# One core, one hybrid block: table powers in PSUM, a table shared with GpSimd, tokens turned unscaled, and the last third of w_mod in column halves

## The chip, the cores and the metric

The kernel runs on one core of a Trainium2 chip. The metric is the device time of one execution in microseconds (us); where several runs were made, their median stands. Beside it there is one profiled execution, whose trace gives every duration that is quoted below. Times "at 83 us" count from the start of that execution's span.

Engines are named as the trace names them: PE is TensorE, DVE is VectorE, ACT is ScalarE, POOL is GpSimd, SP is the engine that here only issues transfers (SPq in the trace).

## The reference, cut to what matters

```python
mod_x = silu(c) @ w_mod + b_mod            # 6 x 1024 values; the same from c_ctx for the context
hx = rmsnorm(x) * (1 + sc1) + sh1          # 256 latent tokens, 256 context tokens, width 1024
ux = hx @ w_in                             # columns 0:512 pooling mixer, 512:1024 SSM
# SSM: 32 groups of 16 channels, 64 complex states, forward and backward, over chunks of 8 tokens
ssm = gelu(readout(scan(ux_ssm)) + d*ux_ssm);  ssm = ssm * sigmoid(ssm @ w_glu + b_glu)
pool = (centred_mean(ux_pool) - ux_pool) @ w_pool * s_pool
x = x + g1 * (concat(pool, ssm) @ w_out)
hx2 = rmsnorm(x) * (1 + sc2) + sh2
eidx, gate = route(hx2)                    # best group of 8 experts, its top 2 of 32 experts in all
x = x + g2 * moe(hx2, eidx, gate)          # w_gate, w_up (1024x512), w_down (512x1024) per expert
return rmsnorm(x) * g_final
```

Everything is float32. The 32 experts' weights are 6 MB each; all of them are read, four experts in each of eight passes.

## The kernel before, in words

Each engine has its own program, written out by hand, and runs it in order; waits on named semaphores order the engines against each other. All large loads go through SP's queue, in the order of SP's program. The work falls into these stages.

**Tables.** The scan over tokens is done in chunks of L = 8 tokens. DVE makes the powers of the 2 x 16 diagonal factors (LP), copies them into PW (a tile of SBUF, `pws`), and multiplies them with the input matrices Br into the table SA and, later and with other powers, with the output matrices CT into the table MO. `powers_times` does this: a table has four parts (direction d, real or imaginary part rr), each made in two halves h, and a half is three instructions over 128x1024 elements: a product into SBUF, a product into PSUM, and the two combined. So SA and MO have eight halves each. POOL makes MO's d = 1, real part, in two halves. PE turns (transposes) SA in sixteen pieces, `turn_sa`, each four 128x128 transposes; ACT copies them into ST (DVE three of them). `lag_kernels(d)` multiplies SA with CT.

**Modulation and first projection.** Meanwhile PE multiplies silu(c) with the first third of w_mod, eight chunks of 1 MB, sums in PSUM bank 4. When all eight are in, ACT copies the row (`mod_rows`), PE turns it, ACT makes columns of it (`mod_columns`), POOL makes the scale A1. PE turns the normed tokens piece by piece (`turn_x`), ACT evacuates each piece with scale and shift into hT, and `u_ssm(q)`, q = 0 to 3, multiplies hT with w_in's SSM half. The turns of x (k = 3 to 7) stand inside `u_ssm(0)`, eight turns of SA inside `u_ssm(1)`.

**States and scan.** `u_evacuate(q)` writes u to DRAM; SP reads it back in another layout (U8, two halves of eight transfers). `state_inputs(0)` and `(1)` multiply it with ST, ACT copies the results, and DVE scans them from then until `hp_ready`. After the last `state_inputs` SP issues w_out's pool half and 15 transfers that build the Toeplitz matrix TT, then the chunks 6 and 7 of w_mod's second third. PE does the pooling projection `u_pool` and the chunks between them, then the windows, w_pool, the Toeplitz product, `mix_pool(0)`, and, with `hp_ready`, the readout y.

**To the residual.** y is copied, turned, put through gelu and the gated unit, and multiplied with w_out (`mix_mm`, four pieces). The last third of w_mod (scale 2, gate 2) is summed on DVE instead of PE: `mod_sum(k)`, one instruction over 128x2048 for each of eight chunks, into `acc`. PE sums acc over the partitions with a matrix of ones, and adds the bias with a second product: the scale half (`scale_mm`) after the second piece of mix_mm, the gate half (`gate_mm`) after the router's logits. From scale_mm DVE makes A2b, the norm's scale, before the first residual.

**Experts.** After the router, `gather` brings tokens to slots. DVE counts passes (`passes_ready`), and each engine loads that number into a register before its loop of four experts. SP's loads of the loop wait until PE has used the buffer. Weights of the first experts are loaded into free buffers before that.

Of the kernel before, what the change touches and what calls it, by code (L numbers as in the profile page):

```python
# [7 lines left out]
ALU = mybir.AluOpType  # L8
# [8 lines left out]
L = 8  # L17
# [41 lines left out]
def hybrid_block(nc, x, ctx, w_mod, columns, ssm_bc, b_mod_rows, w_in, w_out, w_pool, w_glu, w_router, b_router,  # L59
# [14 lines left out]
    with ExitStack() as stack:  # L74
# [22 lines left out]
        pws = sb("pws", 512)  # L97
# [17 lines left out]
        wm0 = wm + [wts[:, 20480:22528], wts[:, 22528:24576], ra[:, 4096:6144], ra[:, 6144:8192], wm[0]]  # L115
# [34 lines left out]
        PW = pws[:, :].rearrange("p (d r g s) -> p d r g s", d=2, r=2, g=GP)  # L150
# [70 lines left out]

        u_dram = nc.dram_tensor("u_scratch", [P, 2048], F32).ap()
# [31 lines left out]
        def _(sp):  # L254
# [55 lines left out]
            sp.dma_start(wglu, w_glu[0].rearrange("(k p) n -> p k n", p=P)).then_inc(S("wglu_in"), 16)  # L310
            sp.dma_start(wo_ssm, w_out_v[:, 4:8, :]).then_inc(S("wo_ssm_in"), 16)
            for k in range(3):
                mod_chunk(2, k)
            sp.wait_ge(S("gff_row"), 16)
            sp.dma_start(gffb, row_dram[1:2, 0:D].broadcast_to([P, D])).then_inc(S("gff_in"), 16)
            sp.wait_ge(S("mod1_row"), 16)
            sp.dma_start(ra[:, 6144:8192], row_dram[0:1].broadcast_to([P, 2048])).then_inc(S("g1_in"), 16)
            sp.wait_ge(S("pool_mm"), 1)
            mod_chunk(2, 3)

            sp.wait_ge(S("hp_ready"), 1)
            mod_chunk(2, 4)
# [3 lines left out]
            mod_chunk(2, 5)  # L326
            gu_load(sp, 0, 0, 0, "up")
            gu_load(sp, 0, 0, 1, "up")
            mod_chunk(2, 6)
            for half in range(2):  # L330
                down_load(sp, lambda j: j, half, (1,))
            mod_chunk(2, 7)
# [3 lines left out]
            sp.wait_ge(S("mod2_used"), KD)  # L336
            gu_load(sp, 0, 0, 0, "gate")
            gu_load(sp, 0, 0, 1, "gate")
# [48 lines left out]
        def _(gp):  # L387
# [21 lines left out]
            gp.wait_ge(S("mod_col"), 1)  # L409
            gp.tensor_tensor(A1, MC[:, 1, :, :], vt[:, V_GM:V_GM + 8].unsqueeze(2).broadcast_to([P, KD, 2]),  # L410
# [1115 lines left out]
```

## Time and profile before

| what | value |
|---|---|
| median of 3 runs | 691.33 us (690.03 to 693.26) |
| the profiled execution, own time | 688.25 us |
| its span in the trace | 686.2 us |
| PE busy | 598.0 us (87%) |
| DVE busy | 210.2 us (31%) |
| ACT busy | 143.5 us (21%) |
| POOL busy | 52.2 us (8%) |
| HBM read | 244.32 MB, 359 GB/s over the span |

How to read it: busy PE is not PE at its peak, since matmuls are pipelined, and a share over the whole span mixes the stages ahead of the experts (about the first 213 us) with the loop of experts (the rest). The chain of work that ended last puts 66% on PE and 20% on DMA. Which of the two limits a stage has to be read from that stage.

### The profile page before, as it was taken

How to read it: one execution, taken by the hardware profiler on the slowest of the kernel's cores; microseconds unless marked ns; L12 is line 12 of the kernel's file. 1: busy time of each engine (PE TensorE's matmuls, PEld its weight loads, DVE VectorE, ACT ScalarE, POOL GpSimd, SP SyncE). 2: the span in 40 equal slices, each digit the busy share in tenths (PEclk: the TensorE clock that was granted, in tenths of full speed). 3: DMA queues.
4: the chain of work that ended last, by engine and by line, in shares of the span. 5: the costliest groups of instructions: out<-in, count | busy, mean ns of one | idle time of the engine just before them, and what ended most of it. 6: DMA issues, size and time to landing. Idle time of an engine off the chain costs nothing.

```text
span 686.2 us, 9304 instructions
## 1 busy us (share of the span) xinstructions
PE 598.0 (87%) x3764; PEld 249.4 (36%) x3764; DVE 210.2 (31%) x427; ACT 143.5 (21%) x229; POOL 52.2 (8%) x90
## 2 busy tenths in 40 slices
PE   1769996879877999799979979997997999799995
PEld 0246452545334334233423423342342333234331
DVE  7996999646663002002000200200020010002003
ACT  7144140130112212210221221021122103111211
POOL 4282900000000000000000000000000000000000
PEclk9989999899977999899999989999998999999998
DMA  8991379999755999999999999999999999999961
GB/s 328 417 380 32 77 275 313 408 400 410 259 205 229 410 421 421 422 422 421 423 422 422 422 422 422 421 422 422 421 422 422 423 420 421 422 423 384 403 235 62
DMA packets 46247, 248.85 MB, mean 363 GB/s; under 512 B 8729, under 2 KB 11433, under 8 KB 18833
## 3 DMA queue, kind: packets, MB, share of 16 engines
q1 hardware_dynamic: 41320, 246.03, 88.3%
q10 hardware_dynamic: 4600, 1.59, 0.9%
q0 software_dynamic: 304, 0.93, 0.6%
q8 instruction: 15, 0.25, 0.1%
q14 instruction: 8, 0.06, 0.0%
HBM read 244.32 MB, written 2.11 MB: 359 GB/s over the span
## 4 chain that ended last, share of the span: by engine, by line
PE 66%; DMA 20%; DVE 7%; SPq 3%; issue 2%; ACT 1%; POOL 0%; DVEq 0%; ACTq 0%; POOLq 0%
PE ps L801 24%; DMA wts<-in_w_up 17%; PE ps L840 16%; PE ps L777 5%; PE ps L771 4%; PE ps L575 4%; DVE rc L1090 3%; PE ps L657 2%; DMA wts<-in_w_mod 1%; PE ps L816 1%; DVE ps L1090 1%; DMA cb<-in_ssm_bc 1%; SPq L303 1%; PE ps L691 1%; PE ps L703 1%
## 5 line engine op out<-in xcount | busy, mean ns | idle before, releaser
L801 PE MATMUL ps<-wts,ra 128*64 128x512 f32 x512 | 243.3, 629 | 35.5 <-DMA wts<-in_w_up 32.2
L802 PE MATMUL ps<-wts,ra 128*64 128x512 f32 x512 | 243.4, 629 | 0.0
L801 PEld LDWEIGHTS ps<-wts,ra 128*64 128x64 f32 x512 | 70.4, 144 | 182.2 <-issue 134.4
L840 PE MATMUL ps<-wts,ra 128*32 128x512 f32 x512 | 111.4, 593 | 0.0
L840 PE MATMUL ps<-rc,ra 128*32 128x512 f32 x512 | 111.4, 593 | 0.0
L1090 DVE TENSOR_TENSOR ra<-ra,ps 128x256 f32<-128x256 f32 x32 | 13.5, 421 | 267.9 <-ACT ra L1041 267.8
L1035 ACT COPY ra<-ps 128x512 f32<-128x512 f32 x32 | 33.6, 1050 | 208.9 <-PE ps L802 208.9
L802 PEld LDWEIGHTS ps<-wts,ra 128*64 128x64 f32 x512 | 70.4, 144 | 0.0
L840 PEld LDWEIGHTS ps<-wts,ra 128*32 128x32 f32 x512 | 29.1, 110 | 73.2 <-issue 73.2
L1090 DVE TENSOR_TENSOR cb<-ps,ra 128x512 f32<-128x512 f32 x32 | 22.1, 692 | 103.4 <-PE ps L840 103.4
L1030 ACT COPY ra<-ps 128x512 f32<-128x512 f32 x32 | 18.6, 585 | 139.0 <-PE ps L771 133.0
L470 POOL TENSOR_TENSOR small<-small 128x1 f32<-128x1 f32 x4 | 2.2, 556 | 508.7 <-DVE small L1473 491.5
L771 PEld LDWEIGHTS ps<-cb,ra 128*128 128x128 f32 x256 | 30.6, 196 | 13.4 <-issue 6.5
L771 PE MATMUL ps<-cb,ra 128*128 128x128 f32 x256 | 33.7, 286 | 0.9 <-ACT ra L1022 0.9
L777 PE MATMUL ps<-cb 128*128 128x512 f32 x68 | 32.9, 606 | 0.0
L575 PE MATMUL ps<-ra,wts 128*128 128x512 f32 x64 | 31.9, 625 | 0.0
L840 PEld LDWEIGHTS ps<-rc,ra 128*32 128x32 f32 x512 | 29.2, 110 | 0.0
L1090 DVE TENSOR_TENSOR ps<-pws,cb 128x1024 f32<-128x1024 f32 x14 | 23.1, 1650 | 0.0
L490 PE MATMUL ps<-wts,sil 128*32 128x512 f32 x80 | 13.0, 736 | 10.4 <-DMA wts<-in_w_mod 10.4
L1090 DVE TENSOR_TENSOR cb<-cst,ut 128x256 f32<-128x256 f32 x16 | 6.7, 421 | 48.9 <-PE ps L771 47.7
L816 PEld LDWEIGHTS ps<-cst,ra 128*128 128x128 f32 x128 | 14.2, 140 | 17.2 <-issue 15.3
L1090 DVE TENSOR_TENSOR rc<-pws,cb 128x1024 f32<-128x1024 f32 x14 | 19.1, 1363 | 0.6 <-DVE pws L1214 0.2
(230 smaller groups left out, 528.0 us busy)
## 6 DMA issues: line engine op xcount, KB each, us to landing
wts<-in_w_up SPq DMA_DIRECT2D x64, 1024.0 KB, 15.5
wts<-in_w_gate SPq DMA_DIRECT2D x64, 1024.0 KB, 13.4
wts<-in_w_down SPq DMA_DIRECT2D x30, 1024.0 KB, 8.7
rc<-in_w_down SPq DMA_DIRECT2D x30, 1024.0 KB, 12.5
wts<-in_w_mod SPq DMA_DIRECT2D x14, 1024.0 KB, 13.7
r<-in_w_mod SPq DMA_DIRECT2D x6, 1024.0 KB, 11.2
wts<-in_w_in SPq DMA_DIRECT2D x2, 2048.0 KB, 23.6
wts<-in_w_out SPq DMA_DIRECT2D x2, 2048.0 KB, 14.5
```

The source lines that it names most:

```text
L490: mm = pe.matmul(ps[32 * j:32 * j + 32, bank, :], silc[:, k, :], w[:, 512 * j:512 * j + 512], start=False, stop=(k == KD - 1))
L575: mm = pe.matmul(ps[:, 4 + q % 3, :], WB[:, k, 512 + P * q:512 + P * q + P], hT[:, k, :], start=(k == 0), stop=(k == KD - 1))
L657: mm = pe.matmul(ps[:, n, :], cat[:, k, P * (n // 2):P * (n // 2) + P], wo_pool[:, k, 512 * (n % 2):512 * (n % 2) + 512], start=(k == 0), ...
L771: mm = pe.matmul(o, h2P[:, t, k, :], Pm[:, t], start=True, stop=True, skip_group_check=True)
L777: mm = pe.matmul(ps[:, 2 * t + h, :], PT[:, t, :], oS[:, 2 * h + t, :], start=False, stop=stop, skip_group_check=True)
L801: pe.matmul(ps[0:64, 4 + b, :], st, Wg[b][:, k, :], start=(k == 0), stop=(k == KD - 1))
L802: mm = pe.matmul(ps[64:128, 4 + b, :], st, Wu[b][:, k, :], start=(k == 0), stop=(k == KD - 1))
L816: mm = pe.transpose(ps[:, 6 + j % 2, P * f:P * f + P], gu[:, j % 2, P * f:P * f + P], ident)
L840: mm = pe.matmul(ps[32 * j:32 * j + 32, BANKS[n], :], hid[:, j, f, SLOTS * t:SLOTS * t + SLOTS], Wd[j][:, f, 512 * h:512 * h + 512], start ...
L1030: act.copy(xm[:, 2 * r:2 * r + 2], ps[:, GATHER[r], :].rearrange("p (k e s) -> p k e s", k=2, e=4)).then_inc(S("xm_ready"), 1)
L1035: act.copy(gu[:, j % 2, :].rearrange("p (f q) -> p q f", f=FC), ps[:, 4 + j % 2, :].rearrange("p (q f) -> p q f", f=FC)).then_inc(S("gu_co ...
L1090: return dve.tensor_tensor(o, a, b, op)
```

## The change

Four things, and what follows from them in the order of work.

1. **Powers in PSUM.** PW is no longer a tile of SBUF but PSUM bank 7. PE's chunks 0 to 2 of w_mod's second third, which also use bank 7, wait for `mo_ready` (all of MO made).
2. **GpSimd makes 3/8 of SA.** POOL makes three of SA's eight halves (d = 1: real h = 1, imaginary h = 0 and 1), straight from LP, with `ut` as scratch; it no longer makes any of MO. DVE makes the other five of SA and all eight of MO. DVE makes A1. ACT copies all sixteen turned pieces. `TURNS` gives the order of the sixteen turns.
3. **Tokens turned unscaled.** `turn_x` for all k stands between w_mod's first eight chunks; ACT copies the pieces plain into hT and applies scale and shift there, in place, once A1 is there. w_mod's chunks 5 and 6 go to other buffers.
4. **Last third of w_mod in halves of columns.** `last_third(j, gate)` loads two chunks of 128 rows, 1024 columns of each; first the four scale halves, then the four gate halves. `mod_sum(k, gate)` works over 128x1024. The bias is added by DVE (`mod_bias`, on one partition), no longer by PE. `scale_mm` stands between `mix_pool(2)` and the gated unit, and DVE makes A2b right after it.

Besides, POOL clears oS and PT instead of DVE; DVE makes `passes_ready` directly after the first slots; ACT takes the first two gathered pieces before it loads its loop count.

```diff
-        PW = pws[:, :].rearrange("p (d r g s) -> p d r g s", d=2, r=2, g=GP)
+        PW = ps[:, 7, :].rearrange("p (d r g s) -> p d r g s", d=2, r=2, g=GP)
+        TURNS = (0, 1, 2, 3, 4, 5, 6, 7, 10, 11, 12, 13, 8, 9, 14, 15)
...
+            gp.wait_ge(S("lp_ready"), 1)
+            gp.wait_ge(S("bbar_ready"), 1)
+            gp.wait_ge(S("ss_ready"), 4)
+            for rr, h in ((0, 1), (1, 0), (1, 1)):
...
+                gp.tensor_tensor(SA[:, 1, rr, g], pr, bi_ if rr else br_, ALU.mult)
+                step(gp.tensor_tensor(t, pi, br_ if rr else bi_, ALU.mult))
+                step(gp.tensor_tensor(SA[:, 1, rr, g], SA[:, 1, rr, g], t, ALU.add if rr else ALU.subtract))
+                gp.sem_inc(S("sa_ready_pool"), 1)
...
+            sp.wait_ge(S("mod_used"), 14)
+            last_third(0, 0)
+            sp.wait_ge(S("mod_used"), 15)
+            last_third(1, 0)
+            sp.wait_ge(S("mod_used"), 16)
+            last_third(2, 0)
             sp.wait_ge(S("u_pool_mm"), NT)
             sp.dma_start(wpool, w_pool[0].rearrange("g c d -> c g d")).then_inc(S("wpool_in"), 16)
...
+            for rr, h in itertools.product(range(2), range(2)):
+                table(SA, Br, 0, rr, h, False, "sa_ready")
+            dve.wait_ge(S("mod_col"), 1)
+            tt(A1, MC[:, 1, :, :], vt[:, V_GM:V_GM + 8].unsqueeze(2).broadcast_to([P, KD, 2]), ALU.mult).then_inc(S("a1_ready"), 1)
+            table(SA, Br, 1, 0, 0, False, "sa_ready")
...
             mix_pool(2)
+            pe.wait_ge(S("scale_sum"), 1)
+            for h in range(2):
+                mm = pe.matmul(ps[:, 6 + h, :], ones, acc[:, 512 * h:512 * h + 512], start=True, stop=True)
+            mm.then_inc(S("scale_mm"), 1)
...
-                if n == 1:
-                    pe.wait_ge(S("mod2_used"), KD)
-                    for h in range(2):
-                        pe.matmul(ps[:, 6 + h, :], ones, acc[:, 512 * h:512 * h + 512], start=True, stop=False)
-                        mm = pe.matmul(ps[:, 6 + h, :], ones[32 * h:32 * h + 1, :], modrow[32 * h:32 * h + 1, 2, :], start=False, stop=True)
-                    mm.then_inc(S("scale_mm"), 1)
...
+                if t == NT - 1:
+
+                    gp.wait_ge(S("gate_mm"), 1)
+                    gp.memset(oS, 0.0).then_inc(S("zeroed"), 1)
```

PE's order around the first projection. Before (L575 is `u_ssm`, L527 a turn of x, L517 a turn of SA), from the last turn ahead of `u_ssm(0)`:

```order
L517 MATMUL ps<-cst,rc 128x128 [waits st_copy_dve]
L517 MATMUL ps<-cst,rc 128x128 x3
L575 MATMUL ps<-ra,wts 128x512 [waits ht_ready,win_ssm_in]
L527 MATMUL ps<-cst,ra 128x128 [waits ht_ready]
L527 MATMUL ps<-cst,ra 128x128 x3
L575 MATMUL ps<-ra,wts 128x512 [waits ht_ready]
```

The same place now (L599 is `u_ssm`, L526 a turn of SA, L508 the turn of the modulation row):

```order
L508 MATMUL ps<-cst,mr 128x128 [waits modrow]
L508 MATMUL ps<-cst,mr 128x128 x3
L599 MATMUL ps<-ra,wts 128x512 [waits ht_ready,win_ssm_in]
L526 MATMUL ps<-cst,rc 128x128 [waits st_copy,sa_ready_pool]
L526 MATMUL ps<-cst,rc 128x128 x3
L599 MATMUL ps<-ra,wts 128x512 [waits ht_ready]
```

The turns of x have left this stretch, and six turns of SA have moved into `u_ssm(0)`; two remain in `u_ssm(1)`, where there were eight.

SP's queue behind w_mod's second third. Before (its columns: line, DMA, where to and from, size; the three rows of w_mod are the last third's chunks 0 to 2):

```order
L283 DMA wts<-in_w_mod 128x2048 [waits mod_used]
L283 DMA r<-in_w_mod 128x2048 [waits mod_used]
L283 DMA wts<-in_w_mod 128x2048 [waits mod_used]
L315 DMA ra<-row_scratch 128x1024 [waits gff_row]
L317 DMA ra<-row_scratch 128x2048 [waits mod1_row]
L283 DMA cb<-in_w_mod 128x2048 [waits pool_mm]
L283 DMA wts<-in_w_mod 128x2048 [waits mod2_used,hp_ready]
```

The stretch from the broadcasts on now:

```order
L323 DMA ra<-row_scratch 128x2048 [waits mod1_row]
L325 DMA ra<-row_scratch 128x1024 [waits gff_row]
L326 DMA wts<-in_w_glu 128x4x512
L288 DMA cb<-in_w_mod 128x2x1024 [waits pool_mm]
L329 DMA wts<-in_w_out 128x4x1024
L244 DMA wts<-in_w_down 128x2048 [waits hp_ready]
L244 DMA wts<-in_w_down 128x2048
L288 DMA wts<-in_w_mod 128x2x1024 [waits mod2_used]
L288 DMA r<-in_w_mod 128x2x1024 [waits mod2_used]
```

w_glu and w_out's second half, which stood ahead of the last third, now stand behind the broadcasts, and one expert's w_down has moved ahead of the gate halves. Three scale halves and w_pool stand ahead of what is shown.

DVE around y and the gated unit (L1365 is ysum, L1369 A2b, L1344 a `mod_sum`), now:

```order
L1365 SCALAR_TENSOR_TENSOR rc<-ut,vt,ps 128x256 [waits y_t]
L1365 SCALAR_TENSOR_TENSOR rc<-ut,vt,ps 128x256 x3
L1369 SCALAR_TENSOR_TENSOR rc<-ps,ra 128x1024 [waits gff_in,scale_mm]
L1341 TENSOR_SCALAR cb<-wts,sil 128x1024 [waits wmod2_in0]
L1344 SCALAR_TENSOR_TENSOR cb<-wts,sil,cb 128x1024 [waits mod2_used,wmod2_in0]
L1344 SCALAR_TENSOR_TENSOR cb<-r,sil,cb 128x1024 [waits mod2_used,wmod2_in1] x2
L1136 TENSOR_TENSOR wts<-rc 128x8x32 [waits sig_ready] x4
```

Before, A2b (L1350) stood behind all eight sums:

```order
L1090 TENSOR_TENSOR wts<-rc 128x8x32 [waits sig_ready] x4
L1312 SCALAR_TENSOR_TENSOR cb<-r,sil,cb 128x2048 [waits mod2_used,wmod2_in5]
L1312 SCALAR_TENSOR_TENSOR cb<-wts,sil,cb 128x2048 [waits mod2_used,wmod2_in6]
L1312 SCALAR_TENSOR_TENSOR cb<-cb,sil 128x2048 [waits mod2_used,wmod2_in7]
L1350 SCALAR_TENSOR_TENSOR rc<-ps,ra 128x1024 [waits gff_in,scale_mm]
L1090 TENSOR_TENSOR ra<-ps,ra 128x1024 [waits dve_link,xres_in0,mix_mm,g1_in]
```

## Rows read from the trace of the kernel before

**Rows 1.** The page: DMA's busy tenths in 40 slices of 17.2 us.
```profile
DMA  8991379999755999999999999999999999999961
```

**Rows 2.** The chain that ended last, in order of time: start us, us, what.
```profile
213.10 1.11 PE ps L801
...
284.11 18.86 DMA wts<-in_w_up
```

**Rows 3.** Windows: from:to, us, busy of each engine, clock, DMA share, GB/s.
```profile
45.00:50.00 5.00, 5.00 (x19) 2.80 (x18) 4.90 (x5) 2.77 (x6) 4.86 (x10) 0.76 1.01 418
```

**Rows 4.** The tile in_w_in: its two transfers, issued at 18.24 and 18.72 us.
```profile
DMA to landing us min/median/max: 21.1/23.6/26.0
```

**Rows 5.** ACT in order of time: start, us, instruction, idle time before it.
```profile
34.38 0.58 ACT L917 COPY mr<-ps 128x512 f32<-128x512 f32 x1 [2.01 <-PE ps L490]
36.64 2.86 ACT L939 ACTIVATE ra<-ps,mcol,aux 128x256 f32<-128x256 f32 x6
```

**Rows 6.** The same chain, first projection.
```profile
43.19 1.71 PE ps L575 x2
...
57.35 0.44 PE ps L517 x4
...
66.87 1.88 PE ps L555 x64
68.75 13.95 PE ps L575 x32
```

**Rows 7.** DVE in order of time, tables.
```profile
19.12 1.23 DVE L1090 TENSOR_TENSOR rc<-pws,cb 128x1024 f32<-128x1024 f32 x1
...
56.43 0.69 DVE L1209 COPY cb<-ps 128x512 f32<-128x512 f32 x1 [5.21 <-PE ps L555]
...
71.80 2.95 DVE L1090 TENSOR_TENSOR ps<-pws,cb 128x1024 f32<-128x1024 f32 x1
74.78 1.22 DVE L1189 SCALAR_TENSOR_TENSOR rc<-rc,ps 128x1024 f32<-128x1024 f32 x1
```

**Rows 8.** POOL in order of time.
```profile
13.47 8.93 POOL L403 TENSOR_SCALAR cb<-cb 64x256 f32<-64x256 f32 x8 [0.62 <-DMA cb<-in_ssm_bc]
...
73.73 3.23 POOL L458 TENSOR_TENSOR rc<-rc,cb 128x1024 f32<-128x1024 f32 x1
```

**Rows 9.** The chain, from the Toeplitz transfers to y.
```profile
110.69 0.60 SPq L304
...
111.96 10.27 DMA wts<-in_w_mod
...
128.22 1.97 PE ps L642 x8
...
138.06 3.73 issue
```

**Rows 10.** The tile in_w_pool, issued at 113.05 us.
```profile
DMA to landing us min/median/max: 10.0/10.0/10.0
```

**Rows 11.** DVE in order of time, from the last third to the router.
```profile
138.32 2.35 DVE L1312 SCALAR_TENSOR_TENSOR cb<-wts,sil,cb 128x2048 f32<-128x2048 f32 x1
...
149.69 1.66 DVE L1323 SCALAR_TENSOR_TENSOR rc<-ut,vt,ps 128x256 f32<-128x256 f32 x4 [9.01 <-PE ps L681]
...
174.40 2.01 DVE L1350 SCALAR_TENSOR_TENSOR rc<-ps,ra 128x1024 f32<-128x1024 f32 x1 [4.38 <-PE ps L710]
...
203.83 0.74 DVE L1090 TENSOR_TENSOR cb<-cb 128x64 f32<-128x64 f32 x3
```

**Rows 12.** The chain again, from the residual to the first expert.
```profile
176.66 1.24 DVE ra L1090
...
204.40 1.05 PE ps L753 x2
...
206.40 0.42 DVE cb L1090
...
212.47 0.59 ACT ra L1030
```

More of the change, by code:

```diff
@@ L325, in _ @@
                 sp.dma_start(x2[:, t, :], x[0, t * P:(t + 1) * P]).then_inc(S(f"xres_in{t}"), 16)
-            mod_chunk(2, 5)
             gu_load(sp, 0, 0, 0, "up")
             gu_load(sp, 0, 0, 1, "up")
[L329 to L332, printed above, removed]
+            sp.wait_ge(S("mod2_used"), 2 * KD)
+            gu_load(sp, 0, 0, 0, "gate")
+            gu_load(sp, 0, 0, 1, "gate")
             sp.wait_ge(S("mix_pool"), 1)
@@ L576, in u_ssm @@
                                    start=(k == 0), stop=(k == KD - 1))
-                    if q == 0 and k < 5:
-                        turn_x(k + 3)
-                    next(turns, None)
+                    if q == 0:
+                        if k in (0, 1):
+                            turn_sa(8 + k)
+                        elif k in (2, 3):
+                            turn_sa(8 + k)
+                        elif k == 4:
+                            lag_kernels(0)
+                        elif k in (5, 6):
+                            turn_sa(7 + k)
+                    elif q == 1 and k in (0, 1):
+                        turn_sa(14 + k)
                 mm.then_inc(S("u_ssm_mm"), 1)
@@ L609, in _ @@
             u_ssm(0)
-            lag_kernels(0)
-            u_ssm(1, itertools.chain(turn_sa(1, 0), turn_sa(1, 1)))
+            u_ssm(1)
             lag_kernels(1)
@@ L631, in _ @@
             pe.wait_ge(S("uP_copy"), NT)
-            pe.wait_ge(S("mo_ready"), 1)
             for g in range(4):
@@ L1222, in _ @@
             dve.wait_ge(S("sa_t"), 16)
-            powers_times(MOv, PW, CT, 1, -1, "mo_half", rs=(1,))
-            dve.wait_ge(S("mo_half"), 3)
-            dve.wait_ge(S("mo_back"), 1)
+            for rr, h in itertools.product(range(2), range(2)):
+                table(MOv, CT, 1, rr, h, rr == 1, "mo_half")
             dve.sem_inc(S("mo_ready"), 1)
@@ L1324, in _ @@
                                          ALU.mult, ALU.add).then_inc(S("ysum_ready"), 1)
-            for k in range(3, 5):
-                mod_sum(k)
+            dve.wait_ge(S("scale_mm"), 1)
+            dve.wait_ge(S("gff_in"), 16)
+            dve.scalar_tensor_tensor(A2b.rearrange("p (k q) -> p k q", k=KD), ps[:, 6:8, :].rearrange("p a (k q) -> p (a k) q", q=P), 1.0,
+                                     gffb.rearrange("p (q k) -> p k q", k=KD), ALU.add, ALU.mult).then_inc(S("a2b_ready"), 1)
+            for k in range(4):
+                mod_sum(k, 1)
             for m in range(4):
```

317 lines of the change are left out of this document (163 added, 154 removed).

## The prediction

> **What bounds the kernel now.** I read the page first. From slice 15 on, all but the last two DMA digits are 9 [rows 1], and the chain waits for a weight of the experts once in each pass [rows 2]: the loop of experts is bound by transfers, its bytes are the same before and after, and its stream can start only when PE has used the first buffers. So the end moves as PE's first expert product moves, which is at 213.10 [rows 2], as long as the weights of the first experts are there by then. Everything that counts lies in the first 213 us, and there the chain in order of time says stage by stage what is late.
>
> The first stage is bound by transfers too: the DMA share is still 1.01 at 45 to 50 us [rows 3], and w_in's SSM half, issued at 18.24, lands 21.1 us later, at 39.3 [rows 4]. PE begins `u_ssm(0)` only at about 43 [rows 6]; between lies DVE, which makes SA without a gap from 19.12 on [rows 7]. From 43 to 82.7 PE is full, and it ends with two pieces of u in 13.95 us [rows 6]. Then u goes to DRAM and back, and when the second half has been multiplied SP issues 15 Toeplitz transfers, the last at 110.69, and w_mod's chunk 7, which lands at 111.96 + 10.27 = 122.2 [rows 9]. PE waits for it. Behind it follow the windows, w_pool's product at 128.22 [rows 9], y, the gated unit and w_out.
>
> The next wait is A2b. DVE has idled 4.38 us for PE's four products of scale and bias and then takes 2.01 us [rows 11]; the residual begins at 176.66 [rows 12]. The last one is the experts' start: the first slots are there at 206.40 + 0.42 = 206.8, but ACT copies the gathered tokens at 212.47 [rows 12], since it and PE wait for the number of passes.
>
> **The change part by part.** Step 1, the front. Four halves of SA on DVE are 12 instructions of 1.22 us: 19.1 + 14.7 = 33.8. Chunk 7 of w_mod's first third now stands behind the turns 6 and 7 (2 x 0.44 [rows 6]), and takes about 1 us: 35.7, where `mod_rows` began at 34.38 before [rows 5]. From there to the first scaled piece it was 36.64 - 34.38 = 2.3 [rows 5]; with the copy of turn 7, 0.6, it comes to 38.7, and the first piece is ready just when w_in is there, 39.3. So `u_ssm(0)` begins 3.7 us earlier. Its pace is then ACT's: two scalings of 0.48 (2.86/6 [rows 5]) and, for four pieces, a copy of 0.6, so piece 4 is ready at 38.7 + 5 x 0.96 + 3 x 0.6 = 45.3. PE needs 0.86 (1.71/2 at the slow clock, 13.95/16 at the full one [rows 6]; I take the full one, since PE now idles only from 37 to 39) for it, 1.88 for `lag_kernels(0)` [rows 6], 3 x 0.87 and two turns for the rest: 51.6. `u_ssm(1)` has two turns instead of eight: 7.9, so 59.5; `lag_kernels(1)` 61.4; and 13.95 more, 75.4, against 82.7. I book 7.0 us earlier.
>
> Three things hide in this. POOL must have its three halves when PE comes to turn 14, one product into `u_ssm(1)`, at 52.5, and ACT's first evacuation, whose target is POOL's scratch, wants them at 51.6. POOL starts at 13.47 + 8.93 = 22.4; nine instructions at the row's 3.23 end at 51.5 [rows 8]. It fits by a hair, and beyond 3.25 each tenth costs 0.9. The row is no lower bound, it ran while DVE worked on two SBUF tensors. By the Trainium skill (GPSIMD Engine Reference, section 3.1) a two-input fp32 instruction of 2048 elements measures 4497 ns there; half of it, as an estimate, would end the tables near 42.6. No run here shows that instruction alone, and the sum would be the same.
>
> Second, MO is now wholly DVE's. From the copy after `lag_kernels(0)` at 48.2: 0.69 [rows 7], 14.7, about 1.0, 14.7, so `mo_ready` is at 79.3. PE wants bank 7 after `state_inputs(0)` and the eight turns, near 81. Slack 1.8; DVE's scan then begins near 81.6 instead of 88.7, so it keeps its lead. Third, a product whose powers lie in PSUM. No row has it. The nearest are 1.22 for an instruction with one PSUM input, made while POOL was at work [rows 7, 8], and, as the upper end, 2.01 for A2b, which also reads PSUM and strided SBUF [rows 11]. I take 1.22, since the patterns of the tables are the same as before and only the memory changes. The pair of rows at 71.80 and 74.78 shows more: a product of two SBUF tensors took 2.95 beside POOL, the combination with PSUM 1.22 beside the same POOL [rows 7]. The new products are of the second kind, so I let neither engine slow the other. The Trainium skill (GPSIMD Engine Reference, section 8) names just these, two SBUF inputs, as contending; the trace agrees with 2.95 against 1.22. Against the change speaks VectorE: DVE Perf Modes, its section on the TRN2 errata, again of the Trainium skill: a PSUM source costs 120 cycles of overhead, an SBUF source 58. That estimate would add 0.065 us to each of 16 products ahead of `mo_ready` and to eight ahead of chunk 7, half a microsecond on the end; the row at 74.78 does not show it.
>
> Step 2, the middle. From u to chunk 7 nothing is changed in order or bytes; all of it moves by 7.0. In what follows I write times as before minus this shift, so chunk 7 lands at "122.2". Behind it stand, new, three scale halves of 1 MB ahead of w_pool. The third is issued only when PE has used chunk 7, and at 418 GB/s [rows 3] a megabyte is 2.5 us: 124.7, 127.2, 129.7, then w_pool, 0.6: "130.4". Before, w_pool landed at 113.05 + 10.0 = 123.0 [rows 10], just behind chunk 7, so the queue does deliver in order. PE wanted it at 128.22 [rows 9]. This costs 2.2 us. The stall of PE within y (3.73 us, "issue" [rows 9]) I leave as it is: the number of products ahead of it is the same.
>
> Step 3, A2b. The four products (1.05 each, as in the gate half [rows 12]) and the 2.26 us to the residual leave the path: 6.4 less. Two products, 2.1, now stand ahead of the gated unit: net 4.3 less. What hides the sums: eight scale halves are 8 x 1.2 (half of 2.35 [rows 11]), from "129.3" on; the fourth pair comes behind 4.5 MB of other loads, near "139"; with two bias additions they end near "143", while the turned y comes at 149.69 + 2.2 [rows 11] and `scale_mm` another 3.4 later. Slack about 12. Of the gate sums four stand ahead of the last input of w_out: ysum ends "153.5", scale_mm "157.3", A2b "159.3", four sums "164.3", the gated unit's sigmoid is ready "165", so 0 to 1 is lost at most, and hidden behind `mix_pool(3)`. Four sums and the bias end near "173", the residual can begin at "174.5". Cover 1.5; without it every microsecond counts. The gate halves of w_mod land from "151" to "159", behind w_down of expert 1.
>
> Step 4, the start of the experts. Two bias products, 2.1, leave ahead of the counts, but the counts also need the choice, there at 203.83 + 0.74 = 204.6 [rows 11], where PE was free at 204.40 + 1.05 = 205.45 [rows 12]. So 0.8. The seven small instructions for the passes follow the slots directly: ready 1.4 after them, at 207.6; DVE's four copies of the table and its load of the count take about 2 more until it frees the banks, 209.7, while POOL clears oS beside it and PE gathers till 209.2. PE then starts at 209.7 instead of 213.1: 2.6 more.
>
> Sum: -7.0 + 2.2 - 4.3 - 0.8 - 2.6 = -12.5. The profiled execution took 688.25, of which 686.2 is span; it becomes 675.8. It lies 3.1 below the median of the runs, so the median becomes 691.33 - 12.5 = 678.8, rounded 679. Expert weights: up, gate and down of the first experts are all issued by then, 10 us and more before use.
>
> **The rivals.** (A) The forecast, with its own range 674 to 684. The terms that are soft: PE's clock at the first expert, up to 2 us less if it is not idle before it, and at `u_ssm(0)`, up to 2.5 us more if the clock falls again as it did there (a pair took 1.71 instead of 0.87 [rows 6]). Chance 0.60.
>
> (B) The queue costs more: the halves of w_mod have rows of 4 KB where a chunk had 8 KB. If they ran at two thirds of 418 GB/s, w_pool would be 3.8 later, and the fourth scale half, w_glu and the gate halves eat their cover: 4 to 5 us, 683. For it: nothing ahead of the first experts is short of bytes except here. Against: w_in with rows of 2 KB is within a share of 1.01 at 418 GB/s. Chance 0.12.
>
> (C) The front gains little: POOL's instructions or ACT's pace hold PE. With POOL at 4.0 us the tables end at 58.4 and 6.8 of the 7.0 are gone: 685.6. With POOL at 4.6 nothing is left of the whole change (no change, 690). For: the 3.23 has no room. Against: it was measured under contention. Chance 0.12 for the first, 0.06 for the second.
>
> (D) Slower. The products with powers in PSUM take 2.01 instead of 1.22. Eight stand ahead of chunk 7 (+6.3) and sixteen more ahead of `mo_ready` (+12.6): it comes at 98.2, PE stands at bank 7 behind it, and so do the second half of the states and the scan. Against the 81 of the forecast that is 17 us, less the 1.8 of turns that PE does meanwhile: +15.4 - 12.5 = +2.9, 694. It decides from a product of about 1.8 us on. For: no row has PSUM read by broadcast with PSUM as output as well. Against: [rows 7], 1.22. Chance 0.10, other losses included.
>
> **How the numbers follow.** The predicted time is that of (A). The range reaches down to 672 (both clock terms in my favour, POOL quick) and up to 688, which takes in (B) and (C) and leaves out the rest of (C) and (D), 0.16. About 0.5%, 3.5 us, is what a measurement of this kernel can tell from no change. Faster: A, B and the first of C, 0.84; I say 0.83. Same 0.07, slower 0.10.
>
> **What would show it.** `u_ssm(0)` begins at 39 to 40 and the last of u ends at 75 to 77. DVE's table instructions with PSUM powers show 1.22 each; a 1.8 proves (D). POOL's nine end before 52, or ACT's first evacuation waits for POOL (C). PE waits about 2 us for w_pool near 121 to 123. A2b lies between ysum and the gate sums, and the residual starts within 1 us of the second mix_mm piece, near 168. PE's first expert product is at 200 to 202. If PE waits there for a weight, or the last sum of the gate half is what the residual waits for, my covers were wrong.

## The result and the profile after

| what | before | changed |
|---|---|---|
| median of 4 runs each, side by side | 690.68 us (689.97 to 693.26) | 681.16 us (679.75 to 684.19) |
| ratio, 95% interval | | 0.9861 (0.9817 to 0.9906) |
| the profiled execution, own time | 688.25 us | 679.75 us |
| its span | 686.2 us | 677.9 us |

The forecast was 679.0 us, its range 672 to 688, and 681.16 us lies inside. The gain is smaller than the forecast, though: 9.5 us by the medians and 8.3 by the two spans, where 12.5 were booked. Two terms were too good by 6.8 us together (w_pool by 4.5, the front by 2.3), and 2.6 came back elsewhere, 2.0 of them from PE's clock, which the sum had left out. That the end fits as well as it does is luck in part. So the rows come stage by stage.

The chain that ended last, first projection (start us, us, what); L599 is `u_ssm`, L580 `lag_kernels`. It answers to [rows 6]:

```profile
40.09 1.65 PE ps L599 x2
...
48.87 1.89 PE ps L580 x64
...
64.03 13.95 PE ps L599 x32
```

`u_ssm(0)` begins at 40.09, at the upper edge of the forecast 39 to 40. The last of u ends at 64.03 + 13.95 = 77.98 instead of 82.70: 4.7 us earlier, where 7.0 were booked. The windows say why the first pairs took 1.6 us and not 0.86 (from:to, us, busy of each engine, granted clock, DMA share, GB/s):

```profile
40.00:42.00 2.00, 1.91 (x5) 0.99 (x6) 1.97 (x2) 0.93 (x2) 1.82 (x5) 0.62 1.05 386
42.00:44.00 2.00, 2.00 (x5) 0.96 (x4) 1.61 (x5) 1.37 (x3) 1.77 (x9) 0.52 1.10 425
44.00:46.00 2.00, 1.91 (x11) 1.13 (x9) 0.00 (x0) 1.57 (x4) 1.81 (x9) 1.00 0.99 413
```

PE had stood still for 2.5 us. The granted clock was still 1.00 when it began again, fell at 40.5 to the lower of two levels (0.50, 1.2 GHz), and was the full one (1.00, 2.4 GHz) only from 44 on.

The tables, in order of time, on DVE and then on POOL, which answer to [rows 7, 8]:

```profile
27.80 1.22 DVE L1136 TENSOR_TENSOR ps<-ps,cb 128x1024 f32<-128x1024 f32 x1
...
38.10 0.65 DVE L1136 TENSOR_TENSOR aux<-mcol,vt 128x16 f32<-128x16 f32 x1 [4.06 <-ACT mcol L966]
```

```profile
21.41 2.04 POOL L436 TENSOR_TENSOR rc<-lam,cb 128x1024 f32<-128x1024 f32 x1 [0.27 <-POOL cb L412]
...
38.80 2.36 POOL L438 TENSOR_TENSOR rc<-rc,ut 128x1024 f32<-128x1024 f32 x1
```

A product with its powers in PSUM takes 1.22 us, as booked, and POOL beside it 2.04 to 2.38 instead of 3.23: POOL's halves are there at 41.2, 14 us before PE turns the first piece that needs the last of them, at 55.1.

The chain again, from chunk 7 of w_mod's second third to y, against [rows 9, 10]:

```profile
107.07 10.80 DMA wts<-in_w_mod
117.92 1.63 PE ps L500 x8
...
119.97 7.97 DMA ra<-in_w_pool
127.99 3.78 PE ps L675 x8
131.77 2.32 PE ps L684 x64
134.09 3.63 PE ps L690 x8
137.72 2.31 PE ps L705 x150
140.04 3.52 issue
```

Up to chunk 7 the lead of 4.7 is kept. Then PE waits 6.5 us for w_pool. Its granted clock, 1.00 up to 124 us, is 0.50 from 126 to 132, so that w_pool's product takes 3.78 where it took 1.97. At 134.09 the lead has become 2.0 us behind (132.07 before): the step cost 6.7, and 2.2 were booked.

DVE at A2b, at the last sum of the gate half, and at the residual, against [rows 11, 12]:

```profile
156.30 2.01 DVE L1369 SCALAR_TENSOR_TENSOR rc<-ps,ra 128x1024 f32<-128x1024 f32 x1 [3.49 <-PE ps L719]
...
170.38 1.38 DVE L1136 TENSOR_TENSOR cb<-cb,mr 1x512 f32<-1x512 f32 x2
...
173.68 1.22 DVE L1136 TENSOR_TENSOR ra<-ps,ra 128x1024 f32<-128x1024 f32 x1 [1.92 <-PE ps L740]
```

The residual waits for PE's second piece of w_out and for nothing else, with a cover of 1.9 us. And the start of the experts in the chain:

```profile
203.02 3.75 PE ps L801 x16
206.78 1.05 PE ps L831
207.83 0.45 PE ps L831
```

It is 6.3 us earlier than the 213.10 of [rows 2]. PE comes without a wait from the gathers, so the clock is up again after one product; the first weights' buffers are freed 8.4 us earlier (SP issues the next load at 210.90 instead of 219.25), and the span is 8.3 shorter.

| step | booked | measured in the two traces |
|---|---|---|
| front, to the last of u | -7.0 | -4.7 |
| w_pool behind three scale halves | +2.2 | +6.7 |
| from mix_pool(0) to mix_pool(2) | 0 | -0.6 |
| A2b, from there to the residual | -4.3 | -4.4 |
| bias, passes, to the first expert | -3.4 | -3.3 |
| clock at the first expert | "up to 2 less" | -2.0 |
| sum | -12.5 | -8.3 |

### The profile page after: what moved, and what is told of

Read it like the earlier page. It is cut to its first block, busy times and chain, and to the rows that moved or that the text cites. A ratio compares the mean times of both kernels' runs of the same rounds, so it can differ in the third digit from the quotient of the medians.

```text
span 677.9 us, 9341 instructions
## 1 busy us (share of the span) xinstructions
PE 588.8 (87%) x3756; PEld 248.5 (37%) x3756; DVE 199.8 (29%) x432; ACT 150.1 (22%) x240; POOL 49.7 (7%) x94
## 3 DMA queue, kind: packets, MB, share of 16 engines
q1 hardware_dynamic: 42344, 246.03, 89.7%
## 4 chain that ended last, share of the span: by engine, by line
PE 64%; DMA 22%; DVE 7%; SPq 3%; issue 2%; ACT 1%; POOL 0%; DVEq 0%; POOLq 0%; ACTq 0%
PE ps L831 22%; DMA wts<-in_w_up 18%; PE ps L870 16%; PE ps L801 5%; PE ps L807 5%; PE ps L599 4%; PE ps L690 2%; DVE rc L1136 2%; DMA wts<-in_w_mod 2%; PE ps L846 1%; DMA ra<-in_w_pool 1%; DVE ps L1136 1%; SPq L310 1%; PE ps L728 1%; PE ps L740 1%
## 5 line engine op out<-in xcount | busy, mean ns | idle before, releaser
L831 PE MATMUL ps<-wts,ra 128*64 128x512 f32 x512 | 240.0, 621 | 33.5 <-DMA wts<-in_w_up 33.5
L832 PE MATMUL ps<-wts,ra 128*64 128x512 f32 x512 | 240.1, 622 | 0.0
L831 PEld LDWEIGHTS ps<-wts,ra 128*64 128x64 f32 x512 | 69.5, 142 | 177.7 <-issue 130.5
L832 PEld LDWEIGHTS ps<-wts,ra 128*64 128x64 f32 x512 | 69.5, 142 | 0.0
L599 PE MATMUL ps<-ra,wts 128*128 128x512 f32 x64 | 31.1, 622 | 2.9 <-ACT ra L980 2.9
L846 PEld LDWEIGHTS ps<-cst,ra 128*128 128x128 f32 x128 | 14.2, 140 | 17.2 <-issue 15.3
L846 PE MATMUL ps<-cst,ra 128*128 128x128 f32 x128 | 18.8, 280 | 0.0
L807 PEld LDWEIGHTS ps<-cb 128*128 128x128 f32 x68 | 11.6, 190 | 15.5 <-issue 14.6
## 6 DMA issues: line engine op xcount, KB each, us to landing
rc<-in_w_down SPq DMA_DIRECT2D x30, 1024.0 KB, 12.5
```

The source lines that it names most:

```text
L599: mm = pe.matmul(ps[:, 4 + q % 3, :], WB[:, k, 512 + P * q:512 + P * q + P], hT[:, k, :], start=(k == 0), stop=(k == KD - 1))
L807: mm = pe.matmul(ps[:, 2 * t + h, :], PT[:, t, :], oS[:, 2 * h + t, :], start=False, stop=stop, skip_group_check=True)
L831: pe.matmul(ps[0:64, 4 + b, :], st, Wg[b][:, k, :], start=(k == 0), stop=(k == KD - 1))
L832: mm = pe.matmul(ps[64:128, 4 + b, :], st, Wu[b][:, k, :], start=(k == 0), stop=(k == KD - 1))
L846: mm = pe.transpose(ps[:, 6 + j % 2, P * f:P * f + P], gu[:, j % 2, P * f:P * f + P], ident)
```

## The experiments

Ratios are to the kernel before, with runs of both on the same chip. Differences between two variants are differences of their ratios, times 690. The intervals are 0.003 to 0.0045 wide on either side, 2 to 3 us, so a smaller difference between two variants rests on the traces. Since one profiled execution can be a microsecond off in the front, traces are compared from the end of the last of u on ("after u").

### 1. w_pool ahead of two scale halves

```diff
             last_third(0, 0)
+            sp.wait_ge(S("u_pool_mm"), NT)
+            sp.dma_start(wpool, w_pool[0].rearrange("g c d -> c g d")).then_inc(S("wpool_in"), 16)
             sp.wait_ge(S("mod_used"), 15)
             last_third(1, 0)
             sp.wait_ge(S("mod_used"), 16)
             last_third(2, 0)
-            sp.wait_ge(S("u_pool_mm"), NT)
-            sp.dma_start(wpool, w_pool[0].rearrange("g c d -> c g d")).then_inc(S("wpool_in"), 16)
```

> The changed kernel with one load moved in the queue of SyncE: w_pool behind the first scale half instead of behind the third. Theory (place in the queue, and PE's clock): w_pool lands near 122.5 to 124.5 instead of 127.94, PE takes it right behind the windows without idling, its products take about 2 us instead of 3.78 and the Toeplitz ones 1.9 instead of 2.3; the median is 5 to 8 us below the changed kernel, 673 to 676. Rival 1 (the bytes, or rows of 4 KB, bound this stretch): what w_pool gains the halves lose, w_pool lands after 126, gain 0 to 2 us, 679 to 681. Rival 2 (the stretch is given back later: the sums of the scale half or the gate half lose their cover): the PE product of w_pool comes 6 us earlier but A2b or the residual do not, gain 1 to 3 us, 678 to 680.

Measured: 675.49 us, ratio 0.9771 (0.9727 to 0.9815), 6.2 us less than the changed kernel. PE in order of time:

```profile
118.77 1.94 PE L500 MATMUL ps<-wts,sil 128*32 128x512 f32 x8 [0.58 <-DMA wts<-in_w_mod]
120.63 3.79 PE L669 MATMUL ps<-cb 128*128 128x128 f32 x16
125.61 1.97 PE L675 MATMUL ps<-cb,ra 128*128 128x256 f32 x8 [1.19 <-ACT cb L1035]
```

PE waits for ACT's copy, not for w_pool, and the product takes 1.97 again. It ends 48.0 us after u instead of 53.8, 5.8 less: the place in the queue was the cause, and rival 1 fell. 1.3 of that is lost on the way to the residual, where `mix_pool(1)` runs at the lower clock (4.92 against 3.63).

### 2. Chunks 6 and 7 amid the Toeplitz transfers

On top of run 1, the two chunks are issued after the sixth Toeplitz transfer instead of after the fifteenth.

> As the run before, and chunks 6 and 7 of w_mod's second third are issued between the Toeplitz transfers (after the sixth of them) instead of behind them. Theory (in front of chunk 7 the time goes into issues of SyncE, not into bytes): chunk 7 is consumed by PE 3 to 5 us earlier than at 119.55, and the median is 3 to 5 us below that of the run before, 668 to 672, until the scan of VectorE becomes what PE waits for. Rival (the Toeplitz transfers are bound by the DMA engines): they land later by what the chunks take, the windows' products wait for them, 0 to 1 us gained or some lost, 673 to 677.

Measured: 673.02 us, ratio 0.9744 (0.9702 to 0.9786), not to be told from run 1. The trace decides: chunk 7 was issued at 104.15, three microseconds earlier, and took 13.21 us to land; PE used it 39.7 us after u, in run 1 39.2. The rival holds: this stretch is full of bytes, and an earlier issue brings nothing.

### 3. The powers back in SBUF

```diff
-        PW = ps[:, 7, :].rearrange("p (d r g s) -> p d r g s", d=2, r=2, g=GP)
+        PW = pws[:, :].rearrange("p (d r g s) -> p d r g s", d=2, r=2, g=GP)
```

> The changed kernel with one edit undone: the powers stand in SBUF again, and GpSimd keeps its three halves of the table. It tests why the products stayed at 1.22 us and GpSimd's table instructions took 2.04 to 2.38 instead of the 3.23 that I had booked. Theory (two engines that both work on SBUF tensors slow each other, a PSUM operand avoids it): VectorE's products whose output lies in SBUF take 2 to 3 us beside GpSimd, GpSimd's go up to 3 us and more, u_ssm(0) begins 3 to 6 us later and the median is 3 to 8 us above the changed kernel. Rival (no contention; the 2.95 and 3.23 of before had to do with their place or strides): VectorE 1.22, GpSimd 2.0 to 2.4, the median within 1 us.

Measured: 690.19 us, ratio 0.9998 (0.9970 to 1.0026): 9.5 us above the changed kernel, more than I had expected. DVE, then POOL:

```profile
23.80 2.67 DVE L1137 TENSOR_TENSOR rc<-pws,cb 128x1024 f32<-128x1024 f32 x1 [0.15 <-DVE rc L1137]
26.39 3.05 DVE L1137 TENSOR_TENSOR ps<-pws,cb 128x1024 f32<-128x1024 f32 x1
29.48 1.22 DVE L1137 TENSOR_TENSOR rc<-rc,ps 128x1024 f32<-128x1024 f32 x1
```

```profile
25.35 3.00 POOL L438 TENSOR_TENSOR ut<-lam,cb 128x1024 f32<-128x1024 f32 x1
28.43 3.21 POOL L439 TENSOR_TENSOR rc<-rc,ut 128x1024 f32<-128x1024 f32 x1
...
45.90 2.35 POOL L439 TENSOR_TENSOR rc<-rc,ut 128x1024 f32<-128x1024 f32 x1
```

Both engines slow down, and only where DVE reads two SBUF tensors: the same POOL instruction takes 3.21 beside such products and 2.35 when DVE is idle, and DVE's combination with a PSUM input keeps its 1.22. The last of u ends at 89.7, 7 us later than before the change; what the rest of the change gains is just used up. Moving the powers is what makes GpSimd's share pay. The Trainium skill (SBUF — State Buffer, SBUF: two separate sides) calls the shared pair of ports an "exclusive lock" that one of the two engines holds for a whole instruction. The trace agrees: DVE's product of 3.05 us ends at 29.44, 1.1 behind POOL's instruction of 25.35, and POOL's next ends at 31.64, 2.2 behind that product. Each takes about what it takes alone, once the other is through; 3.05 is a product of 1.22 and a wait of 1.8.

### 4. PE kept busy ahead of u_ssm(0)

Twenty transposes of the identity into a free PSUM bank, behind the last turn of the modulation row; their result goes unused.

> The changed kernel with 20 turns of the identity into a free PSUM bank in front of u_ssm(0), whose results are used by nobody. Theory (PE came out of a wait with its clock lowered, and u_ssm(0) ran at the lowered clock up to 44 us): the granted clock at 40 to 44 is near full instead of 0.6 and 0.5, the last of u ends 1 to 2 us earlier than at 77.98, the median 1 to 2 us lower, 679 to 680. Rival 1 (u_ssm(0) is paced by ScalarE's pieces and not by PE): the clock is full but u ends when it did, within 0.5 us. Rival 2 (the turns come too late and delay u_ssm(0)): up to 2 us slower.

Measured: 679.26 us, ratio 0.9834 (0.9790 to 0.9877), 1.9 us less, with intervals that overlap. The granted clock is 1.00 from 38 to 46. From the first product to the end of u it took 36.7 us instead of 37.9. But u_ssm(0) began 0.9 later in that execution, since A1 on DVE took 1.25 instead of 0.65. In these profiles A1 takes from 0.32 to 1.26 while POOL makes its tables, and 0.27 in run 6, where POOL makes no table; it, too, reads two SBUF tensors. Inconclusive by itself; see run 12.

### 5. w_out behind w_pool

```diff
             sp.wait_ge(S("s_mm"), 8)
-            sp.dma_start(wo_pool, w_out_v[:, 0:4, :]).then_inc(S("wo_pool_in"), 16)
...
             sp.dma_start(wpool, w_pool[0].rearrange("g c d -> c g d")).then_inc(S("wpool_in"), 16)
+            sp.dma_start(wo_pool, w_out_v[:, 0:4, :]).then_inc(S("wo_pool_in"), 16)
```

> The run with w_pool ahead, and one more load moved: the first 2 MB of w_out go from ahead of the Toeplitz transfers to behind w_pool. Theory (from 88 us to chunk 7 the DMA engines are full, with a share of 0.85 to 1.10 in every stretch, and chunk 7 comes when the bytes ahead of it are through): chunk 7 is used about 5 us earlier after the last of u than the 39.2 us of w_pool ahead, VectorE's scan at 126 is not yet in the way, the median falls by 4 to 5 us against w_pool ahead (675.5), to 670 to 672. Rival 1 (PE's first product with w_out then waits for it): chunk 7 comes 5 us earlier but mix_pool(0) no more than 1 to 2 us earlier. Rival 2 (SyncE's issue of the Toeplitz transfers, some 14 us, sets chunk 7): no gain, 675.

Measured: 668.00 us, ratio 0.9682 (0.9648 to 0.9716), 6.1 us less than run 1, somewhat more than expected.

```profile
111.16 1.06 PE L500 MATMUL ps<-wts,sil 128*32 128x512 f32 x8 [0.35 <-DMA wts<-in_w_mod]
112.16 2.05 PE L669 MATMUL ps<-cb 128*128 128x128 f32 x16
115.40 1.96 PE L675 MATMUL ps<-cb,ra 128*128 128x256 f32 x8 [1.19 <-DMA ra<-in_w_pool]
...
121.47 3.70 PE L690 MATMUL ps<-wts 128*128 128x512 f32 x8 [2.22 <-DMA wts<-in_w_out]
```

Chunk 7 is used 32.5 us after u instead of 39.2, and 2.2 are given back where mix_pool(0) waits for w_out, as rival 1 had it in part. The chunk was also issued 3.9 us earlier, since SP's issues were through sooner; by run 2 an earlier issue alone brings nothing, but here it landed 7.2 us behind its issue instead of 10.0. The surplus is clock: with no long wait ahead of them the chunk's product takes 1.06 instead of 1.94 and the windows 2.05 instead of 3.79. With run 2 this says what limits the stretch: not when a load is issued, but which bytes stand ahead of it.

### 6. No share for GpSimd

DVE makes the three halves as well, behind its own five; the powers stay in PSUM.

> The changed kernel, but VectorE makes GpSimd's three halves of the input table too, behind its own five, with the powers in PSUM. Theory: each half takes 3 x 1.22 and a little, so the first of the three is there near 46 instead of 28 us, the second near 50, the third near 54; the turns of PE inside u_ssm(0) wait for them, 4 to 5 us, and mo_ready comes at 86 instead of 82.4 us: 4 to 6 us slower than the changed kernel, 685 to 687. Rival 1 (GpSimd's share is worth all that the kernel with powers in SBUF lost, 9 us): 690. Rival 2 (the turns have slack, and VectorE idled 7 us from 44 to 51 anyway): 0 to 1 us, 681 to 682.

Measured: 684.82 us, ratio 0.9926 (0.9900 to 0.9951), 4.5 us above the changed kernel. The chain:

```profile
44.65 1.23 DVE rc L1124
45.98 1.11 PE ps L514 x4
47.09 1.71 PE ps L587 x2
```

PE waits at the first turn of d = 1, 4.6 us, for DVE's combination, and the last of u ends 5.5 later. The theory held. With powers in PSUM GpSimd's share is worth 4.5 us; with powers in SBUF (run 3) the kernel that has the share is 5.0 us slower than this one, which has none.

### 7. The tail alone, on the kernel before

```diff
-            dve.memset(PT, 0.0)
-            link(dve.memset(oS, 0.0))
-            dve.sem_inc(S("zeroed"), 1)
+            link(dve.tensor_reduce(best[:, 0:1], ps[:, 5, 2 * NE:4 * NE], AX.X, ALU.max))
...
+            act.wait_ge(S("zeroed"), 2)
             act.sem_inc(S("pt_copy"), 1)
+            act.wait_ge(S("passes_ready"), 1)
+            last_four = act.value_load(pairs[0:1, 0:1], min_val=NE // 4 - 1, max_val=NE - 1)
```

> The kernel before, with one part of the change alone: GpSimd clears oS and PT, VectorE's small instructions for the number of passes follow the slots, and ScalarE copies the first gathered tokens ahead of its wait for that number. The bias products of w_mod's gate stay. Theory (the sum of the prediction, 2.6, and 2 us more because PE's clock does not fall before the first expert): PE's first expert product comes 2.6 us after less than in the kernel before, the median is 2.6 to 4.6 us lower, 686 to 688. Rival (the expert stream's start is set by something else, the weights): the first product moves and the end does not, 690.

Measured: 686.05 us, ratio 0.9936 (0.9911 to 0.9962), 4.4 us less than before. PE:

```profile
209.57 2.74 PE L777 MATMUL ps<-cb,ra 128*128 128x128 f32 x16 [0.89 <-ACT ra L1028]
212.53 1.11 PE L807 MATMUL ps<-wts,ra 128*64 128x512 f32 x1 [0.22 <-DVEq L1437]
...
214.20 0.59 PE L807 MATMUL ps<-wts,ra 128*64 128x512 f32 x1
```

From the residual to the first expert it is 33.4 us instead of 36.4, 3.0 less, where 2.6 were booked, and the products reach their short time after two. The clock adds 1.7 us to that: SP issues the next load 4.5 us behind the first product, where it was 6.2. The median's 4.4 fits the sum of both. In the profiled execution the residual itself began 2.4 us later, so its span is only 1.0 shorter.

### 8. PE kept busy before chunks 6 and 7

On top of run 1, 48 transposes ahead of chunk 6 and 12 ahead of chunk 7.

> The run with w_pool ahead, and 48 turns of the identity into a free PSUM bank while PE waits for chunk 6 and 12 while it waits for chunk 7; nobody uses them. Theory (the wait for chunks 6 and 7 lowers PE's clock, and the last chunk's product and the windows run at half of it, 1.94 and 3.73 us): they take about 1.0 and 1.9 us, 2.5 to 3 us less in all, the median 2 to 3 us below w_pool ahead, 672.5 to 673.5. The gap of PE behind 150 records of y's products, which the trace puts to issue, comes 60 instructions earlier if it hangs on the place in the instruction stream, and stays behind 150 if it hangs on y's operands. Rival: the clock stays up, but VectorE's scan or ScalarE's copy takes over, under 1 us.

Measured: 673.56 us, ratio 0.9759 (0.9722 to 0.9795), 0.8 us below run 1, 1.9 by the medians, and the intervals overlap. In the trace the part is as expected: chunk 7 and the windows take 1.03 and 2.00, 2.6 less, and the residual begins 2.1 us earlier after u. And the gap in y moved:

```profile
129.51 3.29 PE L708 MATMUL ps<-rc,ra 64*32 64x128 f32 x218
136.52 1.50 PE L708 MATMUL ps<-rc,ra 64*32 64x128 f32 x38 [3.72 <-issue]
```

In the changed kernel it lay behind 150 products, and lies behind 218 now. y's operands are the same, so it belongs to the place in the instruction stream; with 60 products added ahead, 150 - 60 + 128 = 218. In run 4, with 20 added, PE stopped for 0.2 us behind 130 = 150 - 20 and for 2.9 behind 258 = 130 + 128 (all of y and two of mix_pool(1)). So there is a mark every 128 products, which are 256 instructions with their weight loads, and in these runs PE stopped for long only at a mark that it reached about 2 us after the one ahead.

### 9. mix_pool(1) amid y

On top of run 5, the eight products of mix_pool(1) stand between y's 128th and 129th.

> The run with w_out behind w_pool, and the eight products of mix_pool(1) stand between the second and the third quarter of y's 256 products instead of behind all of them. Theory (the gap of about 3.8 us within y is PE waiting for its own instructions, of which it used up 128 within 2 us; work of few long instructions amid the short ones covers it): the gap shrinks to under 0.5 us, PE's clock stays full through mix_pool, y ends about 0.2 to 1 us earlier although 3.6 us of other work lie in it, and PE waits about 2 us for the copy of y that mix_pool(1) had covered. The scale of all that: 2 to 3 us for the turned y. The median falls by less, 0.5 to 2 us to 666 to 667.5, since in that run VectorE's sums of the gate half already ended only at 162.8, 0.9 behind PE's second piece of w_out. Rival 1 (the gap belongs to y's operands, or falls again into short instructions): it stays at 3.5 to 4 us and the median at 668 or above.

Measured: 669.39 us, ratio 0.9679 (0.9653 to 0.9705), against 0.9682: nothing gained. PE, then DVE:

```profile
132.61 0.44 PE L707 MATMUL ps<-rc,ra 64*32 64x128 f32 x14
133.28 1.90 PE L707 MATMUL ps<-rc,ra 64*32 64x128 f32 x114 [0.22 <-issue]
```

```profile
138.64 2.67 DVE L1345 SCALAR_TENSOR_TENSOR cb<-cb,sil 128x1024 f32<-128x1024 f32 x2 [4.72 <-DMA cb<-in_w_mod]
...
165.50 1.22 DVE L1137 TENSOR_TENSOR ra<-ps,ra 128x1024 f32<-128x1024 f32 x1
```

The cause of the gap is confirmed: it stands at the same mark, 128 + 8 + 14 = 150, and has shrunk from 3.8 to 0.2 us; y ends 0.2 us earlier after u with 3.6 us of other work inside it. The gain is lost at once, since the fourth scale half and then the gate halves of w_mod are late; the residual starts straight behind DVE's last sum. The forecast of 666 to 667.5 missed.

### 10. Expert 1's w_down behind the gate halves

> The run before, and expert 1's w_down (2 MB) is issued behind the gate halves of w_mod instead of ahead. Theory (the gate halves land 20 us after their issue since 8 MB stand ahead of them, and VectorE's last sums are what the residual waits for): they land 4 to 5 us earlier, the residual begins when PE's second piece of w_out is there, 2 to 3 us earlier, the median 2 to 3 us below the run before, 663.5 to 665. Rival (w_out's second half, or expert weights, are late instead): within 0.5 us of the run before.

Measured: 665.86 us, ratio 0.9626 (0.9597 to 0.9655), 3.7 us below run 9. The residual again waits 1.9 us for PE, as it did in the changed kernel. Theory held; the gap's gain comes out only now.

### 11. ScalarE scales ahead

```diff
-                if 1 <= k <= 4:
-                    copy_st(7 + k)
+                if 2 <= k <= 5:
+                    copy_st(6 + k)
```

> The run before, and in u_ssm(0) ScalarE scales each piece before it copies the turned table of the piece before, where it had waited for PE's turn first. Theory (of the 2.6 us by which the front missed the forecast, a part is ScalarE and PE waiting for each other in turns, 3.2 us for every two pieces): lag_kernels(0) begins 1 to 2 us earlier after the first scaled piece, the last of u 1 to 1.5 us earlier, the median 1 us below the run before. Rival 1 (the lowered clock of PE alone made the difference): no change, within 0.3 us. Rival 2 (the turns now wait for their copies): up to 1 us slower.

Measured: 663.84 us, ratio 0.9597 (0.9568 to 0.9627), 2.0 us below run 10.

```profile
40.20 2.04 PE ps L599 x2
42.24 0.85 PE ps L526 x4
43.09 1.04 PE ps L599 x2
44.13 0.44 PE ps L526 x4
...
48.03 1.88 PE ps L580 x64
```

PE runs without a wait from the first product on, and lag_kernels(0) begins 7.8 us after it, instead of 9.9 in run 10 and 8.8 in the changed kernel, which differ by the clock. At full clock the same edit takes it from 7.5 (run 4) to 6.3 (run 12). So ACT and PE had waited for each other in turns: ACT for a turn that stood behind a product, PE for the piece that ACT had not scaled meanwhile.

### 12. PE kept busy once more, on top of run 11

> The run before (ScalarE scales ahead), with the 20 turns of the identity in front of u_ssm(0) once more. Theory (in the first trial of them the clock stayed up, but ScalarE's order paced u_ssm(0), so it gained about 1 us of what it could; now PE paces it): the first product takes 1.10 instead of 2.04 us and the turn behind it 0.45 instead of 0.85, the last of u ends 1 to 1.5 us earlier, the median 1 to 1.5 us lower, 662.5 to 663. Rival (the front is paced by the scaled pieces all the same): the last of u moves by less than 0.5 us and the median does not.

Measured: 664.01 us, ratio 0.9611 (0.9582 to 0.9641): no gain.

```profile
41.30 1.10 PE ps L599 x2
42.40 0.44 PE ps L526 x4
...
62.75 13.94 PE ps L599 x32
```

The first product and the turn take 1.10 and 0.44, and from there to the end of u it is 35.4 us instead of 36.9: the clock does what the theory says. u_ssm(0) began 1.1 later in this execution (A1 at 1.25 again, and the modulation row 0.5 later), so u ends only 0.4 earlier. PE then waits 1.2 us for w_out (0.7 in run 11), 0.97 at the mark of its own instructions (0.26), and 1.0 for the scale half (0.3). The mark had moved by the 20 turns, to behind 258 products of which 128 + 122 are y's and 8 are mix_pool(1)'s. What is gained in front is not passed on.

## Why the prediction was right, and where its terms were wrong

**What bounds the kernel.** Right: the end moved as PE's first expert product moved, 6.3 and then 2.0 more by the clock of the first experts, 8.3 in span.

**The signs.** DVE's 1.22, POOL's end before 52, A2b's place and the residual right behind PE's second piece came as written. Four did not: the last of u at 77.98 (75 to 77 written), the wait for w_pool of 6.5 us (about 2), the residual at 173.68 (near 168), the first expert product at 206.78 (200 to 202).

**Step 1, the front.** The mechanism was right, the size was off by 2.3 us. "Its pace is then ACT's" counted ACT's durations and not that ACT's copy waits for PE's turn; run 11 got back 1.0 of 1.8 us there, the clock held the rest, which the text had named as a soft term (run 12: 1.5 us). The beginning was 0.8 late.

**POOL at 3.23.** Mis-sized on the safe side: 2.04 to 2.38. The text knew that the row "ran while DVE worked on two SBUF tensors", and yet used it for a stretch in which DVE doesn't. The estimate worked out from the Trainium skill (GPSIMD Engine Reference, section 3.1), 2.25, was nearer; the sum would indeed have been the same.

**Powers in PSUM at 1.22.** Right, and more than it was booked for. I had priced only the risk (D); run 3 shows that without this edit the change gives nothing at all.

**Step 2, w_pool.** The term furthest off: "2.2 us", measured 6.7. I took a megabyte at 418 GB/s from the moment chunk 7 landed. But the third half was issued only at 119.56, when PE had used chunk 7 (the text knew that and did not count it), and from 118 to 128 us the windows show 170, 383, 317, 303 and 217 GB/s, 278 in the mean, at DMA shares of 0.71 to 1.00:

```profile
118.00:120.00 2.00, 2.00 (x13) 0.69 (x14) 1.93 (x5) 0.43 (x1) 0.00 (x0) 0.75 0.75 170
...
126.00:128.00 2.00, 0.01 (x1) 0.01 (x1) 1.89 (x2) 0.00 (x0) 0.00 (x0) 0.50 0.71 217
```

So w_pool's product began 10.1 us behind chunk 7's landing, not 6.0 as before, which is 1.9 more than booked. And a wait of 6.5 us has a second price, PE's clock: 1.8 us in w_pool's product and 0.4 in the Toeplitz product. Another 0.4 was lost at chunk 7 itself. Rival (B) had the place right (w_pool late by more), but not the reason: from 116 to 126 us of run 5, 857 of 993 packets were of 2 to 8 KB, most of them the rows of 4 KB of w_out and the w_mod halves, and 421 GB/s went through at a share of 1.03.

**Step 3, A2b.** Right: 4.4 for 4.3, A2b between ysum and the gate sums, cover 1.9 for 1.5. Runs 5 and 9 show how thin that was: once the middle is 7 us faster, DVE's sums are what the residual waits for.

**Step 4, the tail.** Right: 3.3 for 3.4, and run 7 confirms it alone. The clock gave its full "up to 2 us".

**The rivals.** (D) fell with the first row, 1.22. (C) fell with POOL's 2.04, but its other half, ACT's pace, cost about 1 us (run 11). (A) is what happened, with 4.5 us more lost in the middle than booked and 2 us of clock gained at the end that partly cancel.

## What to carry to other kernels

Where PE waits for a small load, look at what stands ahead of it in the queue before asking when it is issued: changing the order of loads twice gave 12 us here (runs 1 and 5), issuing two of them earlier in the same order gave nothing clear (run 2). Before work is shared with GpSimd, look at whether VectorE's instructions beside it read two SBUF tensors, and put one operand into PSUM if they do. A long wait of PE can cost twice, once in itself and once in the clock that falls with it, and each gain shortens some cover that nobody looked at: after every step, read what the next consumer waits for.

## What the runs showed of the hardware

**PE's own instructions.** A gap in 256 short products, put down to "issue" (3.5 us in the changed kernel, 4.3 at most, in run 2), stands at marks 128 products apart (run 4: 130 and 258, with 0.2 and 2.9 us; run 8: 218; run 9: 150 with mix_pool counted; run 12: 258 with mix_pool counted) and shrinks to 0.2 us when eight long products are put ahead of it (0.97 in run 12, where 122 short ones stood between). The Trainium skill (Runtime: NRT & Kernel Launch, Instruction fetch mechanics) says that instructions come in blocks of 256, and that crossing from one to the next is "mostly hidden"; 128 products with 128 weight loads are such a block. The spacing agrees. "Mostly hidden" does not, where PE gets through a block in 2 us while the DMA engines are full (share 1.02 to 1.04 from 138 to 146 us).

**The clock.** In the changed kernel the granted clock fell half a microsecond after PE had begun u_ssm(0) behind a wait of 2.5 us, and was full again some 4 us after the beginning (0.62, 0.52, 1.00 in the windows above). So the fall can show behind the wait and not in it: in run 5, after 3.1 us, the first product still ran at 1.00 and the next at 0.53. Forty-eight transposes that nobody used kept it at 1.00 from 108 to 116 us of run 8, where PE had waited 6.2 us in the changed kernel.

**Left open.** Why the transfers from 118 to 128 us moved only 278 GB/s was not tried. SP had few of them under way there, and 512 of the 1144 packets were of 512 bytes to 2 KB, as many as w_pool has rows of 512 bytes; either may have a part in it. That PE's gap hangs on the full DMA engines is argued from their share, not shown: no run has the same products with the engines idle. And parts 3 and 4 of the change were not run alone; what they gave is read from the two traces.
